# Cache attention with keys turned by VectorE and scores in eight array tiles

## The chip, the core and the metric

The kernel runs on one core of a Trainium2 chip. The metric is the device time of one execution in microseconds (us), the median of several runs. The engines are TensorE (PE, with its weight loads shown apart as PEld), VectorE (DVE), ScalarE (ACT), GpSimd (POOL) and SyncE (SP); the last two issue the transfers here.

## The reference

The program is one inference step of a two-layer decoder. Layer 0 is a latent attention layer (MLA), layer 1 a recurrent one; both see a prompt of 1024 tokens and eight sequences of eight new tokens. Only one stage of layer 0 is changed: the attention of the eight sampled sequences over their cached keys. Each sequence has 64 pages of 128 keys, found through a page table. A key is a latent row of 256 numbers, which is also its value, and a rotated part of 64.

```python
def mla_scores(q_lat, q_pe, ckv, kpe):
    s = jnp.einsum('bthc,blc->bhtl', q_lat, ckv, preferred_element_type=jnp.float32)
    s = s + jnp.einsum('bthr,blr->bhtl', q_pe, kpe, preferred_element_type=jnp.float32)
    return s * SM_SCALE
...
def attend_sample(q_lat, q_pe, ckv_past, kpe_past, ckv_new, kpe_new):
...
    s_past = mla_scores(q_lat, q_pe, ckv_past, kpe_past)
    s_new = mla_scores(q_lat, q_pe, ckv_new, kpe_new)
...
    p = jax.nn.softmax(jnp.concatenate([s_past, s_new], axis=-1), axis=-1)
...
    return (jnp.einsum('bhtl,blc->bthc', p_past.astype(ckv_past.dtype), ckv_past)
            + jnp.einsum('bhtl,blc->bthc', p_new.astype(ckv_new.dtype), ckv_new))
```

Everything is float32. Eight heads times eight tokens make 64 queries for each sequence.

## The kernel before

The stages of the program run one after the other; the changed one is `decode_attention`. It lies between the attention of the prompt and the output projection, and no engine works on another stage meanwhile. It takes the sequences two at a time, so that 2 x 64 queries fill 128 columns of the array or 128 rows of a result. A loop over the four pairs (Fori, on each engine) holds 17 steps: step 0 for the new tokens, then 16 chunks of 512 keys of each sequence.

POOL loads the pages by indirect transfers (`load`, L983), four for a group of 16 pages of both sequences, into one of two slots; a slot is free when the values of its group are done. Keys lie in a slot with keys on the partitions, and the scores need them with the 256 + 64 components there. So PE turns every key: `keys` (L1164) makes 20 transposes of 128x128 for a chunk, which land in a bank of the accumulation memory; ACT and DVE copy the five blocks of 512 columns from there to `k_T` (`keep_keys`, L1040). POOL first puts the rotated parts of both sequences side by side (L1003), so that they turn together.

In step x, PE does `keys` for chunk x, `turn` for the probabilities of chunk x-1 (L1195, four transposes), the last block of keys, `scores` (L1179 for the rotated part of both sequences, then L1142 four matmuls for the latent part) and `values` for chunk x-1 (L1142 again, eight matmuls). The helper `both` places the matmul of sequence 0 on columns 0 to 63 of the array and that of sequence 1 on columns 64 to 127. DVE takes the maximum of the scores (L1092, L1094, L1096), copies the turned probabilities (L1104) and adds the weighted values to the running sum (L1114, L1117); ACT takes the exponentials (L1059 for the correction, L1061). At the end of a pair the sum is divided (L1132), turned (L1225) and copied (L1072), and after the last pair multiplied with `w_uv` (L1232) and the gate (L1134).

## Time and profile before

| | us |
|---|---|
| median of 3 runs | 1920.43 (1918.05 to 1922.9) |
| span of the profiled execution | 1918.3 |
| around the span, against the median | 2.1 |
| the stage of the change, 776.4 to 1323.8 of the span | 547.4 |
| PE busy in that stage | 504.3 |
| one steady step of it | 7.46 |

The profile is of one execution. "Busy" is the time in which at least one instruction of an engine runs, and the mean duration of an instruction holds its passage through the engine, so a group of overlapping matmuls takes less than the sum of the means. A float32 matmul shows as two records in the trace; a transpose as one.

### The profile page before, as it was taken

How to read it: one execution, taken by the hardware profiler on the slowest of the kernel's cores; microseconds unless marked ns; L12 is line 12 of the kernel's file. 1: busy time of each engine (PE TensorE's matmuls, PEld its weight loads, DVE VectorE, ACT ScalarE, POOL GpSimd, SP SyncE). 2: the span in 40 equal slices, each digit the busy share in tenths (PEclk: the TensorE clock that was granted, in tenths of full speed). 3: DMA queues.
4: the chain of work that ended last, by engine and by line, in shares of the span. 5: the costliest groups of instructions: out<-in, count | busy, mean ns of one | idle time of the engine just before them, and what ended most of it. 6: DMA issues, size and time to landing. Idle time of an engine off the chain costs nothing. (4 is left out here: it accounts for less than half of the span.)

```text
span 1918.3 us, 26899 instructions
## 1 busy us (share of the span) xinstructions
PE 1617.1 (84%) x10091; PEld 1274.6 (66%) x10091; DVE 796.3 (42%) x1403; ACT 627.4 (33%) x1022; POOL 223.0 (12%) x219
## 2 busy tenths in 40 slices
PE   4779996688889798599898998998996999870497
PEld 1379995577777677466555565655875999870285
DVE  1240003364645537255444454544226541239633
ACT  3231212142333324233333332333433232355232
POOL 0000000000000000222222222220121000006121
PEclk7779997799989899699999999998998999995699
DMA  9821100110100000525253245222322111100322
GB/s 333 299 56 45 44 22 24 57 28 1 27 0 27 0 0 0 243 110 220 111 201 143 115 201 217 113 110 80 118 72 64 44 44 33 44 1 0 123 88 77
DMA packets 80578, 169.42 MB, mean 88 GB/s; under 512 B 9941, under 2 KB 51803, under 8 KB 76410
## 3 DMA queue, kind: packets, MB, share of 16 engines
q1 hardware_dynamic: 71290, 84.49, 13.4%
q0 software_dynamic: 9216, 83.89, 10.9%
q8 instruction: 55, 0.90, 0.2%
q14 instruction: 17, 0.14, 0.0%
HBM read 157.91 MB, written 10.45 MB: 88 GB/s over the span
## 5 line engine op out<-in xcount | busy, mean ns | idle before, releaser
L80 PE MATMUL bank<-in_x_hi,in_w_hi 128*128 128x272 f32 x992 | 289.8, 292 | 19.9 <-DVE in_x_lo L413 19.8
L82 PE MATMUL bank<-in_x_hi,in_w_lo 128*128 128x272 f32 x992 | 288.8, 291 | 0.0
L81 PE MATMUL bank<-in_x_lo,in_w_hi 128*128 128x272 f32 x992 | 287.4, 290 | 0.0
L80 PEld LDWEIGHTS bank<-in_x_hi,in_w_hi 128*128 128x128 f32 x992 | 188.6, 190 | 20.5 <-issue 19.8
L81 PEld LDWEIGHTS bank<-in_x_lo,in_w_hi 128*128 128x128 f32 x992 | 188.9, 190 | 0.0
L82 PEld LDWEIGHTS bank<-in_x_hi,in_w_lo 128*128 128x128 f32 x992 | 188.4, 190 | 0.0
L1164 PE MATMUL bank<-c_ident,ckv_pages 128*128 128x128 f32 x1024 | 143.0, 286 | 12.4 <-DMA ckv_pages<-in_cache_ckv,page_parts 12.4
L1040 ACT ACTIVATE k_T<-bank 128x512 f32<-128x512 f32 x192 | 114.3, 598 | 109.8 <-PE bank L1164 109.8
L1164 PEld LDWEIGHTS bank<-c_ident,ckv_pages 128*128 128x128 f32 x1024 | 119.5, 147 | 35.8 <-issue 23.1
L403 DVE TENSOR_TENSOR in_w_lo<-in_w_raw,in_w_hi 128x1024 fp32r<-128x1024 f32 x31 | 37.9, 1224 | 239.2 <-ACT in_w_hi L355 239.1
L1142 PE MATMUL bank<-k_T,q_pair 128*64 128x512 f32 x512 | 124.5, 607 | 0.0
L1142 PE MATMUL bank<-ckv_pages,u_T 128*64 128x256 f32 x1024 | 121.6, 379 | 3.1 <-DVE u_T L1104 3.1
L80 PE MATMUL bank<-out_w_hi,out_g_hi 128*128 128x512 f32 (+1 forms) x288 | 114.8, 398 | 6.5 <-DVE out_w_lo L1391 6.5
L1092 DVE TENSOR_REDUCE d_stat<-bank 128x1 f32<-128x512 f32 x64 | 44.3, 691 | 178.0 <-PE bank L1142 178.0
L1142 PEld LDWEIGHTS bank<-ckv_pages,u_T 128*64 128x64 f32 x1024 | 73.4, 137 | 65.8 <-issue 34.2
L81 PE MATMUL bank<-out_w_lo,out_g_hi 128*128 128x512 f32 (+1 forms) x288 | 113.6, 394 | 0.0
L82 PE MATMUL bank<-out_w_hi,out_g_lo 128*128 128x512 f32 (+1 forms) x288 | 113.5, 394 | 0.0
L355 ACT ACTIVATE in_w_hi<-in_w_raw 128x1024 fp32r<-128x1024 f32 x31 | 32.8, 1059 | 240.2 <-PE bank L82 203.5
L1040 DVE COPY k_T<-bank 128x512 f32<-128x512 f32 x128 | 88.3, 691 | 37.1 <-PE bank L1164 31.7
L1003 POOL TENSOR_TENSOR u_T<-kpe_pages,zero 128x512 f32<-128x512 f32 x64 | 66.3, 1045 | 254.2 <-PE bank L1164 170.9
L823 PE MATMUL bank<-u_T,w_q 128*128 128x272 f32 x384 | 92.3, 401 | 3.1 <-DVE q_lo L739 3.1
L1059 ACT ACTIVATE d_stat<-d_stat 128x1 f32<-128x1 f32 x64 | 18.8, 295 | 228.6 <-DVE d_stat L1096 228.6
(272 smaller groups left out, 2950.4 us busy)
## 6 DMA issues: line engine op xcount, KB each, us to landing
u_T<-in_w_ada SPq DMA_DIRECT2D x12, 2048.0 KB, 14.3
in_w_raw<-in_r_w_in SPq DMA_DIRECT2D x16, 512.0 KB, 3.9
in_w_raw<-in_a_w_in SPq DMA_DIRECT2D x15, 512.0 KB, 4.0
x_tiles<-in_x_prompt SPq DMA_DIRECT2D x8, 512.0 KB, 9.3
out_w_raw<-in_a_w_o SPq DMA_DIRECT2D x8, 512.0 KB, 3.6
out_x_in<-in_x_prompt SPq DMA_DIRECT2D x8, 512.0 KB, 4.0
x_mid<-out_x_new SPq DMA_DIRECT2D x8, 512.0 KB, 2.9
u_T<-in_r_w_o SPq DMA_DIRECT2D x8, 512.0 KB, 8.4
```

What stands on the lines that cost most here:

```text
L80: pe.matmul(out, w_hi, x_hi, start=start, stop=False)
L81: pe.matmul(out, w_hi, x_lo, start=False, stop=False)
L82: return pe.matmul(out, w_lo, x_hi, start=False, stop=stop)
L355: act.activation(w_hi[:, b, :, :], w_raw[:, b, :, :], ACT.Copy).then_inc(w_hi_done, 1)
L403: dve.tensor_tensor(w_lo[:, b, :, :], w_raw[:, b, :, :], w_hi[:, b, :, :].bitcast(F32), ALU.subtract).then_inc(w_lo_done, 1)
L823: mm = pe.matmul(r[:, q, 0:cols], weights(c), x[:, c, cols * q:cols * q + cols], start=(c == 0), stop=(c == nch - 1))
L1003: pool.tensor_tensor(kpe_r[:, c % 2, :, :, :].rearrange("p j s e -> p s j e"), kpe_raw[:, c // 4 % SLOTS, :, 4 * (c % 4):4 * (c % 4) + 4, ...
L1040: ins = eng.activation(dst, src, ACT.Copy) if eng is nc.scalar else eng.tensor_copy(dst, src)
L1059: act.activation(col(CORR, x), col(M, x - 1), ACT.Exp, scale=SCALE, bias=col(NM, x)).then_inc(corr_d, 1)
L1092: dve.tensor_reduce(col(RM), bank[:, S_BANK + x % 2, :], AX.X, ALU.max).then_inc(rmax_d, 1)
L1142: mm = pe.matmul(out[HALF * s:HALF * s + HALF, :], w(s), x(s), start=start, stop=stop, tile_position=(0, HALF * s))
L1164: mm = pe.transpose(bank[:, T_BANK + n % 4, P * j:P * j + P], src, k["ident"][:])
```

## The change

The stage is rewritten; the rest of the program stays, but for the layout of the rotated queries (`a["qpe"]`, which loses its zeros) and the size of a load group.

- **Units.** The work is cut into 32 units, written out without a loop: 1024 keys of each sequence of a pair, eight units for a pair. A group of loads is now eight pages (2 x 1 MB and 2 x 0.25 MB), in one of four slots; the load of unit u waits for the values of unit u-4.
- **Keys.** PE no longer turns keys and nothing copies them out of the accumulation memory. DVE turns them itself: `turn(u, c)`, five instructions of 128x1024 elements for a unit, each of which transposes blocks of 32x32 in place of a whole 128x128. So 32 components of a key stand on 32 partitions, and four sets of 256 keys stand in the four groups of 32 partitions. Units alternate between two buffers, `k_T` and a part of `u_T`.
- **Scores.** With 32 components a matmul fills 32 rows of the array. `scores` runs over ten blocks of 32 components, and in each over the two sequences and the four groups of partitions: 80 matmuls of 32 rows, 64 columns and 256 keys, each on a tile of the array of its own (`tile_position`), eight of them in all. Each group of partitions adds up in its own bank, 0 to 3. The queries stand four times, once in each group of partitions; SP copies them there (`replicate`, 24 transfers for a pair, two pairs ahead).
- **Softmax and values.** One maximum over 1024 scores, one instruction for the running maximum, one exponential over 1024; eight transposes of probabilities, copied by ACT in two halves; 16 matmuls for the values.
- **New tokens** of all pairs are done once, ahead of the units (`o_init`). POOL does no arithmetic. `w_uv` is loaded near the end, after the scores of unit 30.

The core of the diff, added lines alone where the old ones were told above:

```diff
-GP = 16
+GP = 8
...
+            @block.gpsimd
+            def _(pool):
+                for u in range(UNITS):
+                    slot = u % SLOTS
+                    if u >= SLOTS:
+                        pool.wait_ge(pv_done, u - SLOTS + 1)
+                    for s in range(2):
+                        at = a["parts"][:, 2 * u + s:2 * u + s + 1]
+                        for dst, name in ((ckv, "cache_ckv"), (kpe_raw, "cache_kpe")):
+                            pool.indirect_dma_start(dst[:, slot, J * s:J * s + J, :].rearrange("p j c -> p (j c)"), None,
...
+                def exp(u):
+                    act.wait_ge(m_done, u + 1)
+                    if u >= 2:
+                        act.wait_ge(pt_ps, 2 * (u - 1))
+                    act.activation(prob[u % 2].rearrange("p j (a r) -> p a j r", a=4),
+                                   bank[:, 0:4, 0:KEYS].rearrange("p a (j r) -> p a j r", r=32), ACT.Exp,
+                                   scale=SCALE, bias=col(NM, u), accum_out=col(RS, u)).then_inc(e_done, 1)
...
+                def turn(u, c):
...
+                    if c == 0:
+                        dve.wait_ge(raw_in[slot], 64 * (u // SLOTS + 1))
+                        if u >= 2:
+                            dve.wait_ge(s_done, u - 1)
+                    src = ckv[:, slot, :, 64 * c:64 * c + 64] if c < 4 else kpe_raw[:, slot, :, :]
+                    dve.transpose(keys_of(u, 2 * c, 2).rearrange("p b (j r) -> p b j r", r=32),
+                                  src.rearrange("p j (b r) -> p b j r", r=32)).then_inc(kt_d, 1)
...
+                def maximum(u):
+                    dve.wait_ge(s_done, u + 1)
+                    dve.tensor_reduce(col(RM, u), bank[:, 0:4, 0:KEYS], AX.XY, ALU.max).then_inc(rm_d, 1)
...
+                for u in range(UNITS):
+                    maximum(u)
+                    if u + 1 < UNITS:
+                        turn(u + 1, 3)
+                        turn(u + 1, 4)
+                    if u:
+                        accumulate(u - 1)
+                    if u + 2 < UNITS:
+                        for c in range(3):
+                            turn(u + 2, c)
+                accumulate(UNITS - 1)
...
+                    for b in range(BLOCKS):
+                        if b % 2 == 0:
+                            pe.wait_ge(kt_d, STEPS * u + b // 2 + 1)
+                        for s in range(2):
+                            for quad in range(4):
+                                rows = slice(32 * quad, 32 * quad + 32)
+                                mm = pe.matmul(bank[HALF * s:HALF * s + HALF, quad, 0:KEYS], q_rep[rows, pr % 2, b, s, :],
+                                               keys_of(u, b, 1)[rows, 0, KEYS * s:KEYS * s + KEYS], start=(b == 0), stop=(b == BLOCKS - 1),
+                                               tile_position=(32 * quad, HALF * s))
+                    mm.then_inc(s_done, 1)
...
+                scores(0)
+                for u in range(UNITS):
+                    turn(u)
+                    if u + 1 < UNITS:
+                        scores(u + 1)
+                    if u % PER == 0 and u:
+                        turn_out(u // PER - 1)
+                    values(u)
```

On PE, one chunk in the middle of a pair before (L1164 turns keys, first the rotated parts and last three blocks of the next chunk; L1195 turns the probabilities; L1179 and the first L1142 are the scores, the second L1142 the values):

```order
L1164 MATMUL bank<-c_ident,u_T 128x128 x4
L1188 REGISTER_ALU
L1195 MATMUL bank<-c_ident,u_T 128x128 x4
L1156 REGISTER_ALU
L1164 MATMUL bank<-c_ident,ckv_pages 128x128 x4
L1169 REGISTER_ALU
L1170 REGISTER_ALU
L1179 MATMUL bank<-k_T,qpe_pair 128x512
L1142 MATMUL bank<-k_T,q_pair 64x512 x4
L1142 MATMUL bank<-ckv_pages,u_T 64x256 x8
L1154 REGISTER_ALU
L1164 MATMUL bank<-c_ident,ckv_pages 128x128 x12
```

And two units in the middle of a pair after it (L1159 turns the probabilities, L1149 are the scores of an odd and of an even unit, L1170 the values):

```order
L1159 MATMUL bank<-c_ident,u_T 128x128 x8
L1149 MATMUL bank<-k_T,q_rep 64x256 x80
L1170 MATMUL bank<-ckv_pages,u_T 64x256 x16
L1159 MATMUL bank<-c_ident,u_T 128x128 x8
L1149 MATMUL bank<-u_T,q_rep 64x256 x80
L1170 MATMUL bank<-ckv_pages,u_T 64x256 x16
```

For 1024 keys the 40 transposes of keys are gone, and two times five matmuls of scores on whole rows have become 80 on 32 rows; turned probabilities and values are as many as in two chunks.

On DVE, one chunk before:

```order
L1040 COPY k_T<-bank 128x512
L1035 REGISTER_ALU
L1040 COPY k_T<-bank 128x512
L1104 COPY u_T<-bank 128x512
L1086 REGISTER_ALU
L1092 TENSOR_REDUCE d_stat<-bank 128x1
L1093 REGISTER_ALU
L1094 TENSOR_TENSOR d_stat<-d_stat 128x1
L1096 TENSOR_SCALAR d_stat<-d_stat 128x1
L1114 SCALAR_TENSOR_TENSOR d_stat<-d_stat 128x1
L1117 SCALAR_TENSOR_TENSOR o_acc<-o_acc,d_stat,bank 128x256
```

And one unit after it, from its maximum (L1059) on:

```order
L1059 TENSOR_REDUCE d_stat<-bank 128x1
L1062 SCALAR_TENSOR_TENSOR d_stat<-d_stat 128x1
L1054 STREAM_TRANSPOSE k_T<-ckv_pages 128x1024
L1054 STREAM_TRANSPOSE k_T<-kpe_pages 128x1024
L1069 SCALAR_TENSOR_TENSOR d_stat<-d_stat 128x1
L1074 SCALAR_TENSOR_TENSOR o_acc<-o_acc,d_stat,bank 128x256
L1054 STREAM_TRANSPOSE u_T<-ckv_pages 128x1024 x3
```

DVE's copies have gone; behind the maximum of unit u stand the last two turns of unit u+1, the running sum of unit u-1, and the first three turns of unit u+2.

## Rows read from the trace of the kernel before

**Rows 1.** The page's head.

```profile
span 1918.3 us, 26899 instructions
```

**Rows 2.** Busy time by windows: whole stage, one step, a pair's boundary, the start.

```profile
core 0: us, PE busy (x) PEld busy (x) DVE busy (x) ACT busy (x) POOL busy (x), PEclk, DMA share, GB/s
776.40:1323.80 547.40, 504.32 (x3300) 309.96 (x3300) 247.32 (x557) 181.13 (x408) 131.09 (x151) 0.96 0.39 156
840.02:847.48 7.46, 7.46 (x52) 4.55 (x51) 3.70 (x8) 2.92 (x7) 0.00 (x0) 1.00 0.97 413
915.15:934.45 19.30, 12.55 (x71) 7.99 (x72) 5.27 (x16) 3.73 (x10) 7.09 (x8) 0.82 0.69 271
776.40:793.80 17.40, 1.14 (x11) 1.02 (x11) 1.22 (x6) 0.72 (x3) 7.95 (x9) 0.50 0.93 377
```

**Rows 3.** Timeline of one steady step: start, length, engine, line, records.

```profile
840.02 1.53 PE L1164 MATMUL bank<-c_ident,ckv_pages 128*128 128x128 f32 x12
...
842.86 1.10 PE L1179 MATMUL bank<-k_T,qpe_pair 128*128 128x512 f32 x2
...
843.88 1.94 PE L1142 MATMUL bank<-k_T,q_pair 128*64 128x512 f32 x8
...
845.65 1.90 PE L1142 MATMUL bank<-ckv_pages,u_T 128*64 128x256 f32 x16
...
845.87 0.69 DVE L1092 TENSOR_REDUCE d_stat<-bank 128x1 f32<-128x512 f32 x1 [2.72 <-PE bank L1142]
...
847.17 0.67 ACT L1061 ACTIVATE u_T<-bank,d_stat 128x512 f32<-128x512 f32 x1
```

**Rows 4.** Groups by line and shape in the stage: count | busy us, mean ns.

```profile
L1164 PE MATMUL bank<-c_ident,ckv_pages 128*128 128x128 f32 x1024 | 143.0, 286 | 12.4 <-DMA ckv_pages<-in_cache_ckv,page_parts 12.4
...
L1142 PE MATMUL bank<-ckv_pages,u_T 128*64 128x256 f32 x1024 | 121.6, 379 | 3.1 <-DVE u_T L1104 3.1
...
L1092 DVE TENSOR_REDUCE d_stat<-bank 128x1 f32<-128x512 f32 x64 | 44.3, 691 | 178.0 <-PE bank L1142 178.0
L1061 ACT ACTIVATE u_T<-bank,d_stat 128x512 f32<-128x512 f32 x64 | 42.8, 669 | 0.0
...
L1117 DVE SCALAR_TENSOR_TENSOR o_acc<-o_acc,d_stat,bank 128x256 f32<-128x256 f32 x64 | 30.7, 480 | 37.8 <-PE bank L1142 37.8
...
L983 POOL DMA_INDIRECT ckv_pages<-in_cache_ckv,parts_next x28 | 26.8, 956 | 8.0 <-issue 7.7 <-PE bank L1164 0.3
...
L1114 DVE SCALAR_TENSOR_TENSOR d_stat<-d_stat 128x1 f32<-128x1 f32 x64 | 14.0, 219 | 0.0
```

**Rows 5.** Instructions of 128x1024: page groups, then one line's durations (min/median/max).

```profile
L403 DVE TENSOR_TENSOR in_w_lo<-in_w_raw,in_w_hi 128x1024 fp32r<-128x1024 f32 x31 | 37.9, 1224 | 239.2 <-ACT in_w_hi L355 239.1
...
L355 ACT ACTIVATE in_w_hi<-in_w_raw 128x1024 fp32r<-128x1024 f32 x31 | 32.8, 1059 | 240.2 <-PE bank L82 203.5
...
L396 DVE TENSOR_SCALAR xn_T<-xn_T,gs,shift x8: 805/806/809, 111.0 to 123.8; 128x1024 f32<-128x1024 f32 x8
```

**Rows 6.** Transfers in the stage: the queue's share, and us from issue to landing.

```profile
q0 software_dynamic: 9216, 83.89, 38.1%
...
ckv_pages<-in_cache_ckv,parts_next POOLq DMA_INDIRECT x28, 11.1
```

**Rows 7.** Timeline at the stage's start.

```profile
776.44 0.33 SPq L970 DMA_DIRECT2D ckv_new<-out  x1
...
777.26 1.12 POOL L983 DMA_INDIRECT ckv_pages<-in_cache_ckv,page_parts  x1 [0.72 <-POOL zero L975]
...
780.80 0.60 PE L1142 MATMUL bank<-k_new,q_pair 128*64 128x8 f32 x8
...
793.79 0.48 PE L1164 MATMUL bank<-c_ident,ckv_pages 128*128 128x128 f32 x1 [12.38 <-DMA ckv_pages<-in_cache_ckv,page_parts]
```

**Rows 8.** Timeline at the stage's end.

```profile
1311.27 0.19 ACT L1061 ACTIVATION_READ_ACCUMULATOR u_T<-bank,d_stat 128x1 f32 x1
...
1323.08 0.69 DVE L1134 TENSOR_TENSOR u_T<-bank,u_T 128x512 f32<-128x512 f32 x1 [7.19 <-PE bank L1232]
```

More of the change, by code:

```diff
@@ new lines, in decode_attention @@
+        st_new = sb("d_stat_new", [P, 3, PAIRS])
+        st = sb("d_stat", [P, 5, UNITS])
+        l_inv = sb("l_inv", [P, PAIRS])
+        col = lambda row, u: st[:, row, u:u + 1]
+        RM, NM, CORR, RS, LSUM = range(5)
+        raw_in = [sem(f"raw_in{i}") for i in range(SLOTS)]
+        q_in = [sem(f"q_rep_in{i}") for i in range(2)]
+        new_in, wuv_in = sem("new_in"), sem("wuv_in")
+        n_scored, n_masked, n_max, n_neg, n_exp, n_turned, n_kept, n_valued, n_done = (
+            sem("new_" + n) for n in ("scored", "masked", "max", "neg", "exp", "turned", "kept", "valued", "done"))
@@ L1027, in _ @@
-                with pool.Fori(0, NPAIR - 1) as pr:
-                    pair(pr, False)
-                pair(NPAIR - 1, True)
-            def keep_keys(eng, pr, c, mine, done):
-                for b in mine:
-                    n = BLOCKS * c + b
-                    eng.wait_ge(kt_ps, pr * (CHUNKS * BLOCKS) + (n + 1))
-                    if b < 2 and c >= 2:
-                        eng.wait_ge(s_done, pr * STEPS + c)
-                    dst, src = kT[:, c % 2, b, :], bank[:, T_BANK + n % 4, :]
-                    ins = eng.activation(dst, src, ACT.Copy) if eng is nc.scalar else eng.tensor_copy(dst, src)
-                    ins.then_inc(done, 1)
+                                                    bass.IndirectOffsetOnAxis(at, 0)).then_inc(raw_in[slot], 16)
@@ new lines, in _ @@
+                        rows, b = slice(HALF * s, HALF * s + HALF), 2 * pr + s
+                        out, at = bank[rows, NEW_BANK, NTOK * pr:NTOK * pr + NTOK], slice(NTOK * b, NTOK * b + NTOK)
+                        for c in range(VC):
+                            pe.matmul(out, a["qlat"][:, c, b, :], u_T[:, QC + c, NP + NTOK * b:NP + NTOK * b + NTOK],
+                                      start=(c == 0), stop=False, tile_position=(0, HALF * s))
+                        mm = pe.matmul(out, a["qpe"][:, b, :], a["kpe_s"][0:ROPE, at], start=False, stop=True,
+                                       tile_position=(0, HALF * s))
@@ new lines, in _ @@
+                mm.then_inc(n_scored, 1)
+                pe.wait_ge(n_exp, PAIRS)
+                for pr in range(PAIRS):
+                    mm = pe.transpose(bank[0:NTOK, NEW_BANK, P * pr:P * pr + P], p_new[:, pr, :], k["ident"][:])
+                mm.then_inc(n_turned, 1)
+                pe.wait_ge(n_kept, 1)
+                pe.wait_ge(new_in, 16)
+                for pr in range(PAIRS):
+                    for s in range(2):
+                        mm = pe.matmul(bank[HALF * s:HALF * s + HALF, PT_BANK + pr // 2, KVL * (pr % 2):KVL * (pr % 2) + KVL],
+                                       pn_T[:, pr, HALF * s:HALF * s + HALF], ckv_new[:, 2 * pr + s, :], start=True, stop=True,
+                                       tile_position=(0, HALF * s))
@@ new lines, in turn, with values @@
+                def turn(u):
+                    pe.wait_ge(e_done, u + 1)
+                    if u == 0:
+                        pe.wait_ge(n_done, 1)
+                    for j in range(J):
+                        mm = pe.transpose(bank[:, PT_BANK + j // 4, P * (j % 4):P * (j % 4) + P], prob[u % 2][:, j, :], k["ident"][:])
+                        if j % 4 == 3:
+                            mm.then_inc(pt_ps, 1)
+                def values(u):
+                    if u:
+                        pe.wait_ge(o_done, u)
+                    for j in range(J):
+                        if j % 4 == 0:
+                            pe.wait_ge(pt_sb, 2 * u + j // 4 + 1)
+                        for s in range(2):
+                            mm = pe.matmul(bank[HALF * s:HALF * s + HALF, O_BANK, 0:KVL], probT[:, j, HALF * s:HALF * s + HALF],
+                                           ckv[:, u % SLOTS, J * s + j, :], start=(j == 0), stop=(j == J - 1),
+                                           tile_position=(0, HALF * s))
+                    mm.then_inc(pv_done, 1)
@@ L1715, in build @@
             a["qlat"] = own("qlat_T", [P, VC, NB, H * NTOK])
-            a["qpe"] = own("qpe_blocks", [P, NB // 2, P])
+            a["qpe"] = own("qpe_T", [ROPE, NB, H * NTOK])
             a["kpe_s"] = own("kpe_new", [P, NS])
```

369 lines of the change are left out of this document (130 added, 239 removed).

## The prediction

> **What bounds the kernel now.** First the page's head, for the time against which the sum is made: a span of 1918.3 us [rows 1], 2.1 us under the median of the runs, so that I add 2.1 at the end. Then the windows [rows 2]: the stage of the change takes 547.40 us, PE works in 504.32 of them at a mean granted clock of 0.96. In one steady step of 7.46 us PE has no gap at all, at the full clock. There are 64 such steps, 477 us; the other 70 lie at the start (17.4 us, PE idle for 16), at the three boundaries between pairs (19.3 us from the last exponential of a pair to the second step of the next) and at the end. DVE works for 3.70 us of a step and ACT for 2.92, so both have room. Transfers move 413 GB/s in that step, but only 156 over the stage, so they wait for free slots more than the others wait for them.
>
> The timeline of the step [rows 3] shows what PE does in it. Twelve of the 20 key transposes take 1.53 us in one stretch. Less the passage of a single one, 0.29 us [rows 4], they follow each other every 0.11 us; so 20 take 2.2, the four of the probabilities 0.44, the rotated scores 1.0, the latent scores 1.8 and the values 1.8. The sum is 7.2 of 7.46 us, and the rest goes where one kind of work hands over to the next. The values are the row to keep in mind: 16 records, two for each matmul of 256 keys, in 1.90 us. If a record had the array to itself, one would follow each 0.11 us; the trace has two columns of tiles, and the records begin in twos. So (1.90 - 0.17)/8 = 0.216 us is the time of one pass of 256 columns on a tile, with two tiles at work together (0.17 us is the difference between the mean length of a record, 0.38 [rows 4], and that pass).
>
> **PE, one unit of 1024 keys after.** 40 key transposes go, 4.4 us for the two chunks that a unit replaces. Eight transposes of probabilities: 8 x 0.11 = 0.9. Values: 32 records in twos, 16 x 0.216 = 3.46. Scores: 80 matmuls, 160 records with a pass of 0.216 us each. Here no row of before decides, since none shows tiles of fewer than 128 rows side by side. The bounds: all eight tiles together, as the two columns in [rows 3], 20 x 0.216 = 4.32 us; and row tiles that take turns while only the two columns overlap, 80 x 0.216 = 17.28. I take 4.32. The nearest row is that of the values, where tiles with weights, data and result places of their own run side by side; the eight tiles have those too, with four banks, and at each partition two streams of keys are read, as now. Three changes between transposes, scores and values cost about 0.1 us each by what the step of now leaves over (0.26 us for its changes). So PE needs 0.9 + 4.32 + 3.46 + 0.4 = 9.1 us. I take 9.5 us as the period, with 0.4 for waits at hand-overs that are written for no slack.
>
> The Trainium skill, "TensorE: Matmul & The Clock Gate", section "Part 3: Packing small matmuls", says that tiles in rows and columns compose and start some 4 ns apart. By it the price would be the lower bound, 4.32; no run here shows it yet.
>
> **DVE, one unit after.** Copies of keys and probabilities go. Five turns of 128x1024: no row shows this operation. Instructions of that size on operands in SBUF take 1.22 us and 0.81 us [rows 5]; 0.81 is the lower bound, twice the slower one, 2.44, the upper. I take 1.22: the maximum has about that rate too, 0.69 for 512 [rows 4], and the 0.81 is that of one line alone. The maximum: 0.69 for 512 [rows 4], and 1.22 - 0.69 = 0.53 for 512 more. Then 0.22 twice and 0.48. The sum is 5 x 1.22 + 1.22 + 0.92 = 8.2 us, under PE's 9.1, with little room.
>
> **Does the chain of the softmax stay hidden?** PE does the values of unit u-1 (3.5 us) between the scores of u and the turning of its probabilities. In that time lie the maximum (1.22 and 0.2 until it sees the scores), the running maximum 0.22 and the exponential: 0.67 for 512 [rows 4], and as much more as an instruction of ACT takes for 1024, 1.06 [rows 5], so 1.1 to 1.2. With 0.3 of hand-overs this is 3.1 us, hidden by 0.4; without the values over it, it would add 3.1 us to each period, 96 in all. The two turns of unit u+1 behind the maximum are done 4.1 us after the scores, and PE wants their blocks, the last four of ten, more than 6 us after them: hidden. Then three turns of unit u+2 end before the next scores do, some 8.5 of 9.5 us. What is queued behind a late maximum is thus the key turning, on which the next scores wait: should DVE become slower, it becomes the bound itself.
>
> **Transfers.** 83.89 MB in 38.1% of 547.4 us [rows 6] are 402 GB/s, 6.5 us for a unit of 2.62 MB, under 9.5. A load waits for the values of four units before, and its unit is first turned nearly three units after that, against 11.1 us from issue to landing [rows 6]: hidden, by more than a unit. POOL issues four, at 0.96 [rows 4] and some 0.3 between them, 5 us. SP's copies of queries come two pairs ahead; for the first pair 24 issues at 0.33 [rows 7] are 8 us, done about when the first keys land. ACT has 1.2 + 0.3 + 2 x 0.6 = 2.7 us in a unit. The layout of the rotated queries saves two small copies in a loop of the stage ahead: nothing that can be seen.
>
> **The ends of the stage.** Before, the first key transpose starts 16.5 us after the first issue [rows 7], with 5.24 MB on the way, 13.0 us at 402 GB/s, so 3.5 lie around them. With 2.62 MB the keys are there at 3.5 + 6.5 = 10.0 after the issue, 10.9 after the stage's start. DVE then turns five (6.1), copies what the new tokens left (1.2), turns three of unit 1 (3.7), and maximum, running maximum and exponential follow (2.9 with hand-overs): the first exponential ends at 24.8. The boundaries between pairs go, since the units of one pair follow those of the other and the new tokens are done in the first wait. From the end of the last exponential to the end of the gate were 1323.77 - 1311.46 = 12.3 us [rows 8]; four transposes and 16 records more make it 12.3 + 0.4 + 1.7 = 14.4.
>
> **Sum.** 24.8 + 31 x 9.5 + 14.4 = 333.7 us in place of 547.4: 213.7 less. The span comes to 1704.6, the time to 1707. Each us of the period is worth 31 us.
>
> **The rivals.**
>
> *PE can't issue so densely.* 200 records in 9.5 us are one each 0.048 us; the steady step has 52 in 7.46. The only denser stretch is that of 8 records with eight keys each, in 0.60 us [rows 7]; less a passage of 0.29 it is one each 0.045 us, at a granted clock of 0.50, with as many weight loads as matmuls [rows 2]. If that holds for the scores whatever the clock, they take 7.2 us, the period 12.4, the time 1797. Against it: the interval could be half at the full clock.
>
> The Trainium skill has a harder form of it: "TensorE: Matmul & The Clock Gate", section "Part 2: What happens when you issue a matmul", gives about 62 ns for a MATMUL with the hardware decoder off. An estimate by that page alone: 160 x 62 ns = 9.9 us of scores, a period of 15.1 and 1881 us. The row of 0.045 us speaks against it, over eight records.
>
> *Only four tiles work at once*, the row tiles of one sequence and then those of the other, since the matmuls come in that order and a later one can't pass those ahead. Scores 8.64, period 13.8, time 1840. For it: in the step of now the tiles that overlap are neighbours in the order. Against it: nothing but the order speaks for it.
>
> *The turning runs at half rate* (2.44 us): DVE needs 14.3 us, the period 14.6 with a hand-over, time 1865. The first scores of a unit then wait for keys in every unit.
>
> *Row tiles take turns* and only the columns overlap: scores 17.28, period 22.5, time 2110. This is the way to a slower kernel. It decides from a period of 16.4 on, scores of 11.2 us, when fewer than 3.1 tiles are at work on the average. For it: all rows of the trace use the full 128 rows, and none shows row tiles together.
>
> **How the numbers follow.** My forecast 0.60; dense issue 0.13; four tiles 0.08; slow turning 0.07; row tiles in turns, or a mixture beyond the point where it decides, 0.12. The predicted time is 1707. The lower end: a period of 9.0, the bare sum of PE, gives 1691; the upper end reaches over dense issue and four tiles, 1848, and leaves slow turning and row tiles in turns out, 0.19. A measurement of this kernel tells 0.3% (5.8 us) from no change; that is a period within 0.2 us of 16.4, so 0.01. Faster 0.87, slower 0.12.
>
> **What would show it.** In the profile after: windows of one unit at about 9.5 us with PE busy throughout and no boundary between pairs; the scores of a unit, 160 records, in 4.3 to 4.5 us with the first eight starting together (7 us: issue; 8.6: four at once; 17: two); turns at 1.2 us; DVE busy for 8.2 us of a unit; the maximum waiting for PE, not PE for DVE or transfers. It is wrong if PE waits for turned keys, if the scores take more than 6 us, or if the granted clock falls in the scores, which at its lower level would double their passes and the values', a period near 17.

## The result, and the profile after

The change makes the kernel faster, by much less than forecast: 1843.44 us, the median of 4 runs (1839.66 to 1849.57), against 1920.38 for the kernel before on the same chip. The ratio is 0.9607 [0.9586, 0.9628]: 77 us won where 213 were forecast.

The profiled execution, with a span of 1847.4 us, is the slowest of the four (1849.57 us, 6 above the median); the forecast's steps are compared with it.

Windows of the kernel after, in the columns of [rows 2]: the whole stage, a unit near its end, two units that follow each other in its middle, 3.3 us in the scores of the second of them, and the start up to the end of the first exponential.

```profile
778.60:1251.10 472.50, 416.10 (x6508) 268.63 (x6508) 247.24 (x301) 82.19 (x173) 120.94 (x128) 0.89 0.53 187
1222.22:1231.35 9.13, 9.13 (x202) 6.69 (x201) 7.24 (x9) 2.47 (x6) 0.00 (x0) 1.00 0.33 118
945.96:958.85 12.89, 11.62 (x202) 7.61 (x201) 7.48 (x10) 2.76 (x7) 3.79 (x5) 1.00 0.57 206
958.85:973.16 14.31, 13.42 (x202) 8.27 (x201) 7.56 (x10) 2.48 (x6) 3.77 (x5) 0.88 0.51 184
...
963.90:967.20 3.30, 3.30 (x72) 2.76 (x80) 0.00 (x0) 0.00 (x0) 0.00 (x0) 0.54 0.90 360
...
778.60:821.03 42.43, 18.52 (x228) 12.86 (x228) 13.46 (x16) 2.95 (x12) 15.26 (x16) 0.56 0.87 281
```

The unit near the end is the forecast one, 9.13 us without a gap on PE. The two in the middle hold the same 202 records and take 12.89 and 14.31 us. What they have and the first has not is the fifth pair of numbers: POOL, busy for 3.8 us with its loads. All loads are issued by then in the first one. In the second of the two the granted clock is 0.88 in the mean; in 3.3 us of its scores the mean is 0.54, so that it lies at the lower of its two levels (1.2 in place of 2.4 GHz) for nearly all of them.

The timeline of the unit near the end:

```profile
1221.19 1.09 PE L1159 MATMUL bank<-c_ident,u_T 128*128 128x128 f32 x8
...
1222.22 4.57 PE L1149 MATMUL bank<-u_T,q_rep 32*64 32x256 f32 x160
...
1226.72 3.67 PE L1170 MATMUL bank<-ckv_pages,u_T 128*64 128x256 f32 x32
...
1226.90 1.23 DVE L1059 TENSOR_REDUCE d_stat<-bank 128x1 f32<-128x1024 f32 x1 [1.59 <-PE bank L1149]
...
1228.35 1.11 ACT L1018 ACTIVATE u_T<-bank,d_stat 128x1024 f32<-128x1024 f32 x1 [5.38 <-DVE d_stat L1062]
```

By the starts, transposes take 1.03 us, scores 4.50 and values 3.60 (the next transposes begin at 1230.32). The 160 records of the scores end 4.57 us after the first began; less the passage of the last (0.37) that is 4.20, or 0.026 us each. They start in groups of eight, some 7 ns apart within a group (the eight of the first between 1222.22 and 1222.26), and most groups follow each other every 0.216 us. The maximum begins 0.11 us after the scores, and the exponential ends at 1229.46, 0.9 us before the values do.

The same stretch of the first unit in the middle:

```profile
945.29 0.94 POOL L1001 DMA_INDIRECT ckv_pages<-in_cache_ckv,page_parts  x1 [10.24 <-PE bank L1170]
945.46 3.49 DVE L1054 STREAM_TRANSPOSE k_T<-ckv_pages 128x1024 f32<-128x1024 f32 x3
...
945.96 2.84 PE L1149 MATMUL bank<-u_T,q_rep 32*64 32x256 f32 x54
946.54 0.95 POOL L1001 DMA_INDIRECT kpe_pages<-in_cache_kpe,page_parts  x1 [0.30 <-issue]
...
947.79 0.94 POOL L1001 DMA_INDIRECT ckv_pages<-in_cache_ckv,page_parts  x1 [0.30 <-issue]
...
949.04 0.95 POOL L1001 DMA_INDIRECT kpe_pages<-in_cache_kpe,page_parts  x1 [0.30 <-issue]
949.58 1.11 PE L1149 MATMUL bank<-u_T,q_rep 32*64 32x256 f32 x5 [0.78 <-issue]
...
951.02 3.27 PE L1149 MATMUL bank<-u_T,q_rep 32*64 32x256 f32 x101 [0.33 <-issue]
```

PE waits for nothing that the profile can name ("issue"). It gets through some 48 records, then only a dozen in 3.4 us, then 101 at full rate. This slow stretch begins 2.3 us after POOL's first issue and ends 1.0 us after the last (949.99 to 951.02). It is PE's alone: DVE's three turns beside it take 3.49 us, as in the quiet unit (3.49). The scores become 7.9 us long, 3.7 more.

The durations on DVE, by line and shape:

```profile
L1054 DVE STREAM_TRANSPOSE k_T<-ckv_pages 128x1024 f32<-128x1024 f32 x64 | 75.6, 1220 | 0.0
...
L1059 DVE TENSOR_REDUCE d_stat<-bank 128x1 f32<-128x1024 f32 x32 | 39.2, 1224 | 193.1 <-PE bank L1149 193.1
```

The timeline of the start, which answers to [rows 7], and the last exponential:

```profile
778.99 3.69 SPq L976 DMA_DIRECT2D q_rep<-qlat_T  x4
...
791.11 1.02 PE L1128 MATMUL bank<-c_ident,p_new 128*8 128x128 f32 x4 [6.02 <-issue]
791.52 4.62 DVE L1054 STREAM_TRANSPOSE u_T<-ckv_pages 128x1024 f32<-128x1024 f32 x4 [1.74 <-DMA kpe_pages<-in_cache_kpe,page_parts]
...
798.22 0.59 ACT L1012 ACTIVATE p_new_T<-bank 8x512 f32<-8x512 f32 x1 [7.17 <-remote]
...
810.92 7.41 PE L1149 MATMUL bank<-u_T,q_rep 32*64 32x256 f32 x160 [8.38 <-DMA q_rep<-qpe_T]
...
819.91 1.11 ACT L1018 ACTIVATE u_T<-bank,d_stat 128x1024 f32<-128x1024 f32 x1 [21.10 <-DVE d_stat L1062]
...
1237.48 1.11 ACT L1018 ACTIVATE u_T<-bank,d_stat 128x1024 f32<-128x1024 f32 x1 [5.38 <-DVE d_stat L1062]
```

From the first exponential to the last are 417.6 us, 31 periods of 13.47. The stage is then 42.4 + 417.6 + 12.5 = 472.5, where 24.8 + 294.5 + 14.4 were forecast: 123.1 us too much in the periods, 17.6 at the start, 1.9 too little at the end. The other 4 of the 142.8 us between this span and the forecast one (1704.6) lie outside the stage.

The periods themselves, from exponential to exponential, are 8.42 for the first, 9.20 and 9.13 for the last two, and 12.8 to 16.0 for the 28 in which POOL issues loads. Those 28 take 390.8 us, 135 more than 28 x 9.13. A stall of 3.72 in each is 104. Seventeen of them are longer still, fifteen by some 1.6 us (14.3 to 14.5) and two by 3.2: 30 together. The two are units 8 and 16, each the first of a pair; unit 24, the first of the last pair, is not among them (12.86). In these seventeen windows the granted clock is 0.88 or, in the two, 0.79; in all others it is 1.00.

### The profile page after: what moved, and what is told of

Read it like the earlier page. It is cut to its first block and busy times, and to the rows that moved or that the text cites. A ratio compares the mean times of both kernels' runs of the same rounds, so it can differ in the third digit from the quotient of the medians.

```text
span 1847.4 us, 31351 instructions
## 1 busy us (share of the span) xinstructions
PE 1528.8 (83%) x13299; PEld 1234.3 (67%) x13299; DVE 795.2 (43%) x1138; ACT 529.4 (29%) x787; POOL 212.8 (12%) x196
## 5 line engine op out<-in xcount | busy, mean ns | idle before, releaser
L1001 POOL DMA_INDIRECT ckv_pages<-in_cache_ckv,page_parts x64 | 60.4, 944 | 961.0 <-POOLq L1658 669.4
L1149 PE MATMUL bank<-k_T,q_rep 32*64 32x256 f32 x2560 | 132.7, 462 | 14.9 <-issue 11.8
L1149 PE MATMUL bank<-u_T,q_rep 32*64 32x256 f32 x2560 | 120.9, 418 | 23.2 <-issue 11.7
L1018 ACT ACTIVATE u_T<-bank,d_stat 128x1024 f32<-128x1024 f32 x32 | 35.6, 1114 | 319.3 <-DVE d_stat L1062 319.3
L1149 PEld LDWEIGHTS bank<-k_T,q_rep 32*64 32x64 f32 x2560 | 82.8, 164 | 60.1 <-issue 48.8
L1059 DVE TENSOR_REDUCE d_stat<-bank 128x1 f32<-128x1024 f32 x32 | 39.2, 1224 | 193.1 <-PE bank L1149 193.1
L1149 PEld LDWEIGHTS bank<-u_T,q_rep 32*64 32x64 f32 x2560 | 74.8, 145 | 65.3 <-issue 49.0
L1170 PE MATMUL bank<-ckv_pages,u_T 128*64 128x256 f32 x1024 | 117.6, 382 | 0.3 <-ACT u_T L1029 0.3
L1170 PEld LDWEIGHTS bank<-ckv_pages,u_T 128*64 128x64 f32 x1024 | 71.1, 137 | 43.8 <-issue 11.9
L819 PEld LDWEIGHTS bank<-u_T,w_q 128*128 128x128 f32 x384 | 75.4, 198 | 20.6 <-DVE q_lo L737 4.8
```

What stands on the lines that cost most here:

```text
L819: mm = pe.matmul(r[:, q, 0:cols], weights(c), x[:, c, cols * q:cols * q + cols], start=(c == 0), stop=(c == nch - 1))
L1001: pool.indirect_dma_start(dst[:, slot, J * s:J * s + J, :].rearrange("p j c -> p (j c)"), None, io[name][0].rearrange("n (q j) c -> (n q) ...
L1018: act.activation(prob[u % 2].rearrange("p j (a r) -> p a j r", a=4), bank[:, 0:4, 0:KEYS].rearrange("p a (j r) -> p a j r", r=32), ACT.Exp ...
L1059: dve.tensor_reduce(col(RM, u), bank[:, 0:4, 0:KEYS], AX.XY, ALU.max).then_inc(rm_d, 1)
L1149: mm = pe.matmul(bank[HALF * s:HALF * s + HALF, quad, 0:KEYS], q_rep[rows, pr % 2, b, s, :], keys_of(u, b, 1)[rows, 0, KEYS * s:KEYS * s + ...
L1170: mm = pe.matmul(bank[HALF * s:HALF * s + HALF, O_BANK, 0:KVL], probT[:, j, HALF * s:HALF * s + HALF], ckv[:, u % SLOTS, J * s + j, :], st ...
```

## The experiments

Theory A: the issue of an indirect transfer by GpSimd holds up TensorE's supply of matmuls, so the stall goes with the number of such issues and with where they fall. What else those 28 units share are the transfers in flight, and the order of the matmuls; on these the rivals rest. Line numbers shift a little between kernels, and units count from 0. Where a kernel ran once, its time is of that run alone, and the reading rests on its trace.

One more rival can be settled in the trace of the kernel after. Its stage is written out without a loop, so more instructions have to be brought in, by transfers on a queue of their own (`q8 instruction` in the profile, 71 packets in place of 55). They don't make the stall: the scores of unit 20 (1085.77 to 1094.09) last 8.3 us like those of its neighbours, and between 1085.7 and 1094.1 only the queue of the loads starts any transfer:

```profile
q0 software_dynamic: 416, 2.49, 78.1%
```

**The same bytes by SyncE** (e1_direct). POOL's block is gone; SP issues plain transfers in its place.

```diff
-                        at = a["parts"][:, 2 * u + s:2 * u + s + 1]
+                        at = P * (2 * u + s)
...
-                            pool.indirect_dma_start(dst[:, slot, J * s:J * s + J, :].rearrange("p j c -> p (j c)"), None,
...
+                            sp.dma_start(dst[:, slot, J * s:J * s + J, :].rearrange("p j c -> p (j c)"),
...
```

> This kernel leaves the gather out: SyncE loads the same number of bytes at the same points of the program by plain transfers, from pages in the order of memory and not of the page table; GpSimd issues nothing. Theory A (while GpSimd issues indirect transfers, instructions reach TensorE too slowly for the dense scores): no stall is left, the scores take 4.2 us in every unit, the period is 9.2 to 9.6 us in place of 13.5, and the span falls by 110 to 130 us to about 1725. Theory B (the data that land hold TensorE up): the stall of 3.4 us stays in every unit with a load, the period stays near 13.5. Theory C (the scores are too dense for the instruction supply in any case): as B.

Measured: 1754.79 us (one run). The scores of one unit, and those of another in two parts, with the transfers of the instruction queue that start between 862.5 and 863.8 (one, of 0.02 MB):

```profile
899.23 4.57 PE L1146 MATMUL bank<-k_T,q_rep 32*64 32x256 f32 x160
...
859.66 4.13 PE L1146 MATMUL bank<-k_T,q_rep 32*64 32x256 f32 x140
...
865.17 1.08 PE L1146 MATMUL bank<-k_T,q_rep 32*64 32x256 f32 x20 [1.38 <-issue]
...
q8 instruction: 1, 0.02, 4.7%
```

The scores take 4.20 us in 24 of the 32 units, beside as many bytes in flight, and the period is 9.13 in ten of them. The mean is 10.44: two units take 18 us (loads queue behind the query copies on SP), several others 10 to 12. So the stall that every loading unit had is gone, and the time lies above the expected one for other reasons. One of them I hadn't seen: in units 3, 5, 10 and 19 PE breaks off in the midst of the scores for about 2 us, though GpSimd issues nothing in this kernel. Each break ends 1.3 to 1.5 us after a transfer of the instruction queue has landed (for the one above 863.76, then 865.17), so PE seems to wait for its next instructions there. e11_three_and_one breaks off at the same records of the same four units.

**Two of four issues** (e2_two_issues). Only the latent rows come by indirect transfers; SP fetches the rotated ones.

```diff
-                        for dst, name in ((ckv, "cache_ckv"), (kpe_raw, "cache_kpe")):
+                        for dst, name in ((ckv, "cache_ckv"),):
```

> GpSimd issues two indirect transfers for a unit in place of four (the latent rows); the rotated rows are loaded by SyncE with plain transfers, in the order of memory, so that this part of the gather is left out. Bytes and points of the program stay. Theory A: GpSimd's issues last 2.2 us in place of 4.7, so the stall shrinks by 2.5 us to about 0.9, the scores take about 5.1 us, the period some 10.2. Theory B: the stall stays at 3.4 us and the period near 13.5.

Measured: 1755.08 us (one run). Timeline of one of its units:

```profile
845.19 0.94 POOL L1012 DMA_INDIRECT ckv_pages<-in_cache_ckv,page_parts  x1 [7.87 <-PE bank L1182]
...
845.86 5.50 PE L1161 MATMUL bank<-k_T,q_rep 32*64 32x256 f32 x160
846.43 0.93 POOL L1012 DMA_INDIRECT ckv_pages<-in_cache_ckv,page_parts  x1 [0.30 <-issue]
```

The scores take 5.50 us to their last end in place of 4.57: a stall of 0.9 as expected, with 80% of the indirect bytes still there. The period is 10.05 in most units, 10.19 in the mean.

**Six issues** (e3_six_issues). Two small ones are added to each load.

```diff
+                        pool.indirect_dma_start(spare[:, (2 * u + s) % 2, :], None,
+                                                io["cache_kpe"][0].rearrange("n (q j) c -> (n q) (j c)", q=8 * PPP),
+                                                bass.IndirectOffsetOnAxis(at, 0)).then_inc(spare_in[s], 16)
```

> Two more indirect transfers for each unit, of 256 bytes for each partition into a spare tile that nobody reads: the bytes grow by 1 per cent, GpSimd's issues from 4.7 to 7.2 us. Theory A: the stall grows by 2.5 us to about 5.9, the scores to about 10 us, the period by 2.5 us or more to 16 and above, the span by some 75 us. Theory B: the stall stays at 3.4 us, the period near 13.5.

Measured: 1941.11 us (one run), slower than the kernel before. Timeline, the first and the last issue and the scores:

```profile
899.78 0.94 POOL L1006 DMA_INDIRECT ckv_pages<-in_cache_ckv,page_parts  x1 [9.98 <-PE bank L1178]
...
900.45 3.27 PE L1157 MATMUL bank<-u_T,q_rep 32*64 32x256 f32 x55
...
906.02 0.94 POOL L1009 DMA_INDIRECT spare<-in_cache_kpe,page_parts  x1 [0.30 <-issue]
...
908.37 4.63 PE L1157 MATMUL bank<-u_T,q_rep 32*64 32x256 f32 x92 [0.29 <-issue]
```

The slow stretch now reaches to 908.4, 1.4 us after the last issue, and the 92 records behind it need 4.3 us, where 2.4 would do: the granted clock of this period is 0.80. The scores take 12.2 us, some 6 of them stall and 1.9 the low clock, and the period is 17.0, 3 us over the mean of the kernel after (13.96). Two issues with hardly a byte do that: it is their number, not what they move.

**Order of the tiles** (e6_order). The sequences alternate inside each group of partitions.

```diff
-                        for s in range(2):
-                            for quad in range(4):
+                        for quad in range(4):
+                            for s in range(2):
```

> The kernel of the change with the matmuls of a block in the other order: for each group of partitions first the one sequence, then the other. If the order of the tiles matters (a later tile can't pass those ahead, or weight loads of one row group get in each other's way), the scores of the units without loads change from 4.2 us, by up to a factor of two. If all eight tiles run together in either order, they stay at 4.2 us, the stall at 3.4 and the span at 1840 to 1850.

Measured: 1854.75 us (one run), periods mostly of 12.85 and 14.4 as before, a few near 16 (13.67 in the mean), and 4.20 us of scores in a unit without issues. The order is no cause.

**Plain transfers by GpSimd** (e8_pool_plain). The engine that issues, the queue and the bytes stay; the gather goes.

```diff
-                            pool.indirect_dma_start(dst[:, slot, J * s:J * s + J, :].rearrange("p j c -> p (j c)"), None,
...
+                            pool.dma_start(dst[:, slot, J * s:J * s + J, :].rearrange("p j c -> p (j c)"),
...
```

> The kernel of the change with GpSimd issuing plain transfers in place of indirect ones, at the same points and with the same bytes, from pages in the order of memory, so that the gather is left out. If it is the indirect transfer whose issuing slows TensorE's instructions, the scores take 4.2 us and the period is near 9.2 but for waits on loads, as in e1_direct. If anything that GpSimd issues does it, the stall stays, near 3 us for a unit.

Measured: 1728.78 us (one run). Timeline of one unit:

```profile
941.49 0.53 POOL L1001 DMA_DIRECT2D ckv_pages<-in_cache_ckv  x1 [7.02 <-PE bank L1170]
...
942.13 4.57 PE L1149 MATMUL bank<-k_T,q_rep 32*64 32x256 f32 x160
...
943.06 0.54 POOL L1001 DMA_DIRECT2D kpe_pages<-in_cache_kpe  x1
```

Four issues at the start of the scores, and the scores are undisturbed, here and in all but two of the units with loads (3 and 10, which break off as in e1_direct): it is the indirect form that counts. That these four are over sooner (2.1 us in place of 4.7) isn't the reason: the two indirect ones of e2_two_issues, 2.2 us, cost 0.9. The period is 9.13 in most units, 9.60 in the mean.

**Issues behind the scores** (e4_late). A load also waits for the scores of unit u-2, so that its issues lie beside values and transposes. Its keys come later, so DVE turns all of unit u+1 behind the maximum of u.

```diff
+                        pool.wait_ge(s_done, u - 1)
...
-                        turn(u + 1, 3)
-                        turn(u + 1, 4)
+                        for c in range(STEPS):
+                            turn(u + 1, c)
```

> The load of a unit waits for the scores of unit u-2 also, so that GpSimd issues during the values and not during the scores; and VectorE turns all of unit u+1 behind the maximum of unit u, so that the later landing is not waited for. Everything is computed. Theory A: the stall moves into the values and the turning of the probabilities, whose instructions come four times less densely; 0 to 1.5 us are left in the scores, the period is 9.3 to 11, the time 1715 to 1765. Theory B: the data still land during the scores, up to 9 us after the first issue, so the stall stays, and the period near 13.5. Theory C: period near 13.5.

Measured: 1764.87 us (1762.54 to 1767.53), ratio 0.9199 [0.9173, 0.9224]. Timeline:

```profile
943.91 3.67 PE L1166 MATMUL bank<-ckv_pages,u_T 128*64 128x256 f32 x32
...
944.76 0.95 POOL L1002 DMA_INDIRECT ckv_pages<-in_cache_ckv,page_parts  x1 [5.91 <-PE bank L1145]
...
948.52 0.95 POOL L1002 DMA_INDIRECT kpe_pages<-in_cache_kpe,page_parts  x1 [0.30 <-issue]
948.54 1.16 PE L1145 MATMUL bank<-k_T,q_rep 32*64 32x256 f32 x29
...
950.49 4.11 PE L1145 MATMUL bank<-k_T,q_rep 32*64 32x256 f32 x131 [0.79 <-issue]
```

Only the last issue reaches into the scores: 1.5 us of stall, a period of 10.61 in most units, and a granted clock of 1.00 in all periods but two (0.99 and 0.88). The values, 32 records in 3.67 us beside the first issues, lose nothing.

**Issues from the sixth block on** (e5_mid). As e4_late, but with the wait on a signal in the midst of the scores, so that the tail of the scores' records might cover them.

```diff
+                        pool.wait_ge(s_mid, u - 1)
...
+                        if b == 5:
+                            mm.then_inc(s_mid, 1)
```

> As e4_late, but GpSimd's wait is raised by the sixth of the ten blocks of the scores and not by the last, some 1.7 us earlier. Theory A, sized by e4_late (issues began 0.85 us after the scores and 1.5 us of stall were left in the next scores): the slow supply then ends before the next scores begin, and what comes slowly are values and turned probabilities, which need few instructions; 0 to 0.3 us of stall are left, the period is 9.1 to 9.6 in most units, the time 1715 to 1740. A rival to it, that the scores always lose about 1.5 us when loads are under way: period as in e4_late, 10.6, time near 1765.

Measured: 1852.74 us (1839.24 to 1855.56), ratio 0.9636 [0.9596, 0.9676], a mean period of 13.55. Timeline of one unit:

```profile
968.77 5.15 PE L1145 MATMUL bank<-u_T,q_rep 32*64 32x256 f32 x160
...
972.97 0.94 POOL L1002 DMA_INDIRECT ckv_pages<-in_cache_ckv,page_parts  x1 [9.91 <-PE bank L1145]
...
976.71 0.95 POOL L1002 DMA_INDIRECT kpe_pages<-in_cache_kpe,page_parts  x1 [0.30 <-issue]
...
978.78 1.23 DVE L1060 TENSOR_REDUCE d_stat<-bank 128x1 f32<-128x1024 f32 x1 [7.04 <-remote]
```

**A new start** (e7_start). SP and ACT share the query copies of the first pair, the loads of units 1 to 3 wait for them, and the second pair's copies come later.

```diff
-                replicate(0)
-                replicate(1)
+                replicate(0, sp, (0, 1))
+                sp.wait_ge(s_done, 2)
+                replicate(1, sp)
...
+                    if u == 1:
+                        pool.wait_ge(q_in[0], 16 * 24)
...
+                replicate(0, act, (2, 3))
```

> The kernel of the change with another start: the copies of the queries of the first pair are issued half by SyncE, half by ScalarE, those of the second pair wait for the scores of unit 1, and the loads from unit 1 on wait for the copies of the first pair. If the late start (first exponential 42 us after the stage's start in place of 25) comes from these copies queueing behind four units of loads and at 0.6 us each on SyncE, the first scores start some 15 us earlier and the span is 10 to 17 us shorter. If it comes from the instruction supply of the cold start, the start stays within 3 us.

Measured: 1842.49 us (one run, beside 1917.43 for the kernel before), no gain on the kernel after. This trace's stage starts at 775.25, 3.4 us earlier than that of the kernel after, so times are counted from the stage's start. The first scores start 17.4 us earlier (at 790.18), but take 20.5 us: twelve issues, 790.27 to 804.96, now run beside them. The first exponential ends 4.0 us earlier. So the late queries were a cause of the long start, and the issues take most of the gain back.

**Both together** (e9_late_start): the edits of e4_late with the new start; only the loads of units 0 and 1 are issued at once.

```diff
+                    if u >= 2:
+                        pool.wait_ge(s_done, u - 1)
```

> As e4_late, with another start: only the loads of units 0 and 1 are issued at once, from unit 2 on each waits for the scores of unit u-2; the copies of the first pair's queries are issued half by SyncE and half by ScalarE, those of the second pair after unit 1. Everything is computed. By theory A the sixteen issues at the start hold the first scores up as they do later (in e7_start the first scores began 21 us earlier and then took 20 us instead of 7): with eight issues, over before the first keys land, the first exponential ends 15 to 23 us earlier than in e4_late and the time is 1740 to 1752. If the start is bound by the first keys and the cold clock alone, it gains under 5 us.

Measured: 1752.67 us (1751.91 to 1763.24), ratio 0.9153 [0.9130, 0.9177]. The first exponential ends at 807.25, counted from the stage's start 12.7 us earlier than in e4_late (820.35); this and the time fall just short of the expected. Timeline of its start:

```profile
791.61 1.02 PE L1126 MATMUL bank<-c_ident,p_new 128*8 128x128 f32 x4 [8.09 <-ACT p_new L1012]
792.66 0.59 ACT L1015 ACTIVATE p_new_T<-bank 8x512 f32<-8x512 f32 x1 [1.10 <-PE bank L1126]
```

With POOL's issues over (the last ends at 787.79), ACT follows PE's four transposes by 0.03 us. In the kernel after, with issues up to 799.26, it followed the same four by 6.1 us (792.13 to 798.22): the late signal of e5_mid once more.

**Two and two** (e10_two_and_two): the latent issues behind the scores of u-2, the rotated ones behind the values of u-3.

```diff
+                    for dst, name in ((ckv, "cache_ckv"), (kpe_raw, "cache_kpe")):
+                        if dst is kpe_raw and u >= 3:
+                            pool.wait_ge(pv_done, u - 2)
```

> As e9_late_start, but the four issues of a unit are parted: the latent rows wait for the scores of unit u-2 as there, the rotated rows for the values of unit u-3, after which the next scores come. By theory A two issues behind the scores cost nothing or some tenths (slow until 4.4 us after the scores, the next scores begin at 4.6), two ahead of the scores 0.9 us as in e2_two_issues: the period is 10.1 to 10.5 in place of 10.6, the time 3 to 15 us under that of e9_late_start. If each issuing of transfers has a fixed cost, however many issues it has, the period grows to 11 or more.

Measured: 1744.94 us (1743.6 to 1751.62), ratio 0.9100 [0.9077, 0.9123]. The scores take 5.12 us and the period is 10.05 in the undisturbed units, 10.51 in the mean: the second pair reaches into the scores as the two of e2_two_issues did.

**Three and one** (e11_three_and_one): three behind the scores, the fourth alone, at the second block of the scores.

```diff
+                            if dst is kpe_raw and s == 1 and u >= 2:
+                                pool.wait_ge(s_mid, u)
...
+                        if b == 1:
+                            mm.then_inc(s_mid, 1)
```

> As e10_two_and_two, but three issues follow the scores of unit u-2 (both latent rows, the rotated rows of one sequence), and the fourth stands alone in the scores of unit u-1, raised by the second of their ten blocks. Everything is computed. If a burst of n issues holds the scores up for about its length (1.25 n - 0.3 us) less 1.3 us that what TensorE already has covers (n = 2: 0.9, n = 4: 3.4, n = 6: 5.9, as e2, the change and e3 fit), a single issue costs nothing even in the scores, and three behind the scores end before the next have used up what is there: the period is 9.1 to 9.5 in most units, the time 1710 to 1725. If every burst costs 0.5 to 0.9 us whatever its length, the period stays at 10.0 or above, the time at 1740 or more.

Measured: 1740.55 us (1736.44 to 1749.0), ratio 0.9078 [0.9058, 0.9098], the best of these, if not to be told from e10_two_and_two. Timeline:

```profile
911.54 5.27 PE L1149 MATMUL bank<-k_T,q_rep 32*64 32x256 f32 x160
...
913.02 0.95 POOL L1005 DMA_INDIRECT kpe_pages<-in_cache_kpe,page_parts  x1 [1.81 <-PE bank L1149]
```

The three cost nothing now, but the one in the scores costs 0.70 us (5.27 against 4.57), and the period is 9.83 where nothing else comes in between, more than expected. In the mean it is 10.37, for several units also have the breaks seen in e1_direct; so mean and time fall where the rival had them (10.0 and 1740 or more), though three in a burst cost nothing and one alone 0.7. I had taken it that an issue's first us is covered wherever it falls. At the start of the scores the slow stretch came 2.3 us after the first issue, here, in their midst, 1.0 us after it. That TensorE has matmuls taken in ahead at the start and none to spare in the midst is a guess; no run shows it.

## Why the prediction was right or wrong

**The step that failed** is the paragraph on transfers. It costs POOL's four issues, "at 0.96 and some 0.3 between them, 5 us", at nothing, as an engine with time to spare. Their duration was right (0.94). What was missing is that they hold up TensorE: 3.72 us in each of 28 units, 104 us, and 30 more in the longer units. The experiments show the cause so far: indirect issues, not transfers (e1_direct), not the issuing engine (e8_pool_plain), not the tiles' order (e6_order); it grows with their number (0.9, 3.7 and some 6 us for two, four and six) and shrinks when they are moved (e4_late, e10_two_and_two, e11_three_and_one).

The kernel before couldn't show it. There a group of four issues (833.65 to 838.35) lies in a step of 7.62 us between exponentials, and the next takes 7.29: 14.91 for two, as much as without issues.

```profile
832.26 0.67 ACT L1061 ACTIVATE u_T<-bank,d_stat 128x512 f32<-128x512 f32 x1
...
833.65 0.98 POOL L983 DMA_INDIRECT ckv_pages<-in_cache_ckv,parts_next  x1 [0.35 <-issue]
...
837.42 0.93 POOL L983 DMA_INDIRECT kpe_pages<-in_cache_kpe,parts_next  x1 [0.31 <-issue]
...
839.88 0.67 ACT L1061 ACTIVATE u_T<-bank,d_stat 128x512 f32<-128x512 f32 x1
```

But PE had 52 records in 7.46 us [rows 2], not 160 in 4.2. By this reading the change made a harmless load into a costly one without touching its kind, only by supplying PE more densely beside it. The density is argued, not shown: the steps before also run in a loop, the units after are written out, and no run parts the two.

**The low clock** was named as what would make the forecast wrong, "if the granted clock falls in the scores". It fell, for about 3.3 us, behind the stall. But 11 of the 28 units have the stall at a granted clock of 1.00 throughout, so the low clock isn't what makes it. In e4_late, whose stall is 1.5 us, the clock stays at 1.00 in all periods but two; it follows the longer stall, and adds the 30 us above to it.

**The start** was 17.6 us too short. It set 24 copies at 0.33 us each, by the one SP issue of [rows 7], 8 us in all; on the chip four take 2.57 and two 1.23, so 0.6 each, where nothing holds them up. And they share the transfer engines with four units of loads, so that PE waits until 810.92 for queries when its first keys are turned at 797.3; from 799.8 to 811, when all of the first pair's copies are issued, the loads' queue takes 93.7% of the engines' time. e9_late_start gives back 13 us of the start.

**Right** were the terms of the sum on PE: 9.1 forecast, 9.13 measured; scores 4.32 against 4.40 (4.57 less 0.17, as the prediction counts; 4.20 is from the first start to the last), and the records start in groups of eight, so all eight tiles work together. The Trainium skill, "TensorE: Matmul & The Clock Gate", section "Part 3: Packing small matmuls", says that tiles in rows and columns compose; the trace agrees: all 160 records take 4.40 us. Only the starts, some 4 ns apart by that section, lie 7 ns apart here, and the measurement decides. The turns take 1.22 us as taken from [rows 5], the maximum 1.22, and the chain of the softmax 2.7 from the end of the scores, hidden by 0.9. The end took 12.5 against 14.4, as long as before (12.3): what the four more transposes and 16 records were to add doesn't show. Two slips change nothing: the bare sum of PE, 9.1, stands as 9.0 at the range's lower end, and not all rows of the trace before use the full 128 rows (the values of the new tokens use 8).

**The rivals.** Four tiles at a time, turning at half rate, and row tiles in turns are all refuted by the 4.20 us and the 1.22. So is dense issue at 0.045 us a record: at the full clock it is 0.026. The Trainium skill, "TensorE: Matmul & The Clock Gate", section "Part 2: What happens when you issue a matmul", gives some 62 ns for a MATMUL with the hardware decoder off; the trace has less than half of that for a record, so that case isn't this one. That the time came out near the rival of four tiles (1840) is chance: its mechanism is not there. It is luck, too, that the time lies in the stated range (1691 to 1848), whose upper end was set by that rival and by dense issue. The real mechanism was in no rival, and the prediction's key for the length of the scores (7 us: issue; 8.6: four at once) would have led to the wrong one, for they took 7.9; the units without loads, and the shape of the stall, told it apart.

**What stays open.** By which path the indirect issues hold up TensorE's instructions and signals. The Trainium skill, "DMA: Bandwidth & Descriptors", section "SWDGE vs HWDGE vs iDMA", says that GpSimd builds its descriptors in software and writes them into SBUF; but it says so of plain and indirect ones alike, and the plain ones of e8_pool_plain disturb nothing here. Open too: why the clock falls in 17 of the 28 units and not in all, and why units 8 and 16 are the longest.

## What to carry to other kernels

An engine that only issues transfers isn't free because it is idle otherwise: look at what the densest stretch of TensorE does while indirect transfers are issued, and put those issues behind it, where fewer instructions and no awaited signal suffer. A trace that shows no cost for an operation shows it for that density of instructions alone; when a change makes matmuls smaller and more, cost again what runs beside them. When copies feed the first matmul of a stage, look at the order in which queues land them, not at their issue alone.

## What the runs showed of the hardware

- Indirect issues of GpSimd slow TensorE's matmuls in a dense stretch: from 2.3 us after the first until 1.0 us after the last, some 12 records in 3.4 us in place of 130 (four issues, kernel after). A single one in the midst costs 0.7 us (e11_three_and_one), plain ones nothing (e8_pool_plain).
- They also delay TensorE's signals to other engines, by 4.9 us (e5_mid) and 6.1 us (at the start), while DVE's own work runs on undisturbed (three turns in 3.49 us beside issues and without).
- Eight tiles of 32 rows by 64 columns work together: 80 float32 matmuls of 256 columns, two records each, in 4.20 us from the first start to the last, at the full clock.
- An indirect issue takes 0.94 us, whether it moves 32 KB (e3_six_issues), 256 KB or 1 MB; a plain one of the same rows by GpSimd 0.53, and a query copy by SP 0.6.
- In a program without a loop PE breaks off now and then, it seems for want of instructions: in e1_direct four times for about 2 us in the scores, each break ending 1.3 to 1.5 us after a transfer of the instruction queue.
